# Feed-forward down product: rounds of 2, 2, 2, 2, 3 pairs of feature tiles, operands fetched a round ahead, the residual added by GpSimd

## Chip, cores and metric

One core of one Trainium2 chip runs the whole program. The metric is the device time of one launch in microseconds, lower is better. The trace gives a duration and a releaser for each instruction; TensorE is called PE, VectorE DVE, ScalarE ACT, GpSimd POOL and SyncE SP, as in the trace. SP computes nothing here: it only issues transfers (DMAs), in the order of its program.

## What is computed

The reference is one step of an encoder trunk for 1152 tokens (1024 of a prompt and 8 x 16 of samples) with a model width of 1024. It begins and ends with a half-step feed-forward network:

```
def half_ffn(x, g, w_up, w_down):
    a, b = jnp.split(rmsnorm(x, g) @ w_up, 2, axis=-1)
    return x + 0.5 * ((jax.nn.silu(a) * b) @ w_down)

x <- half_ffn(x, norm_ffn1, ...)
x <- x + token_mix(rmsnorm(x))          # attention and matrix memory, not touched by the change
x <- half_ffn(x, norm_ffn2, ...)
y  = rmsnorm(x)
```

D_FF is 2816, so the hidden layer has 22 tiles of 128 features. The kernel's function `ffn` runs twice; its tensors begin with f1 in the first run and f2 in the second. The change touches both alike.

## The kernel before

**Products.** Every f32 operand is split into a high part and a low remainder, and one product is three matmuls (`product3`, L515 to L519). On top of that a 2 x 2 block product is done with 7 block products instead of 8 (a Strassen scheme). The 1152 tokens form two halves of HT = 576 columns. A tile of weights n therefore has 7 *steps* q = 0 to 6 on PE; each step multiplies one weight block ("slot") by one operand `xd[r, q]` for all 576 columns.

**Up and down.** 22 up tiles come first (n = 0 to 21). They give 11 groups g, each a pair of feature tiles. DVE and ACT pack the 7 operands of each group into `stg` and SP stores them to `h_dram`. Then come 20 down tiles (n = UPS + m, UPS = 22, m = 0 to 19) in five *rounds* of four. All four tiles of a round read the same operands, those of the groups in `ROUNDS[r]`; tile m yields the output rows k = 2(m % 4) and k + 1 of `xT`. Before the change round 0 takes three groups (18 matmuls a step) and the others two (12 matmuls a step). At the end of each step DVE adds the block times 0.5 to `xT` (`accumulate`, L922), which frees the PSUM bank for a later step (`free_bank`): step 4 of tile m = 0, for example, may start when three evictions are done (`dn_ev`).

**Weights.** Per slot ACT writes the high part (`split_hi`, L754) and GpSimd the low part (L872). Four slots are held, so slot x of a tile can be split once PE has done the step four before it. Four of the seven slots need a term that DVE computes (`weight_term`, L893) from the raw weights `raw_d`, of which two tiles are held. `load_raw(n)` on SP therefore waits for the low part of slot 6 of tile n - 2:

```
def load_raw(n):
    sp.wait_ge(lo_ok, slot_no(n - 1, 0))
```

**Order.** Each engine walks the steps in one order written by hand. The tables `RAW_AT`, `LO_AT` (stores), `LOAD_AT` (operands) and `Y_AT` say at which step SP issues what. All is in program order, so an SP wait holds back all later transfers, and a DVE or GpSimd wait all its later work.

**Memory and residual.** The memory of the up operands is 14 pieces of 9216 bytes per partition. An operand of two groups takes one piece, one of three groups one and a half (K3). The input x of the network is saved to `r_dram` at the start, since `xT` serves as scratch during the up stage; `load_y` brings it back in four transfers of 1.18 MB straight into `xT`, and DVE waits for them (`y_in`) before it adds the first block of tiles m = 0 to 3.

Of the kernel before, what the change touches and what calls it, by code (L numbers as in the profile page):

```python
# [20 lines left out]
ALU = mybir.AluOpType  # L21
# [3 lines left out]
P = 128  # L25
# [6 lines left out]
N_TOK = SEQ + DEC_BATCH * DEC_SEQ  # L32
# [4 lines left out]
HT, QT = N_TOK // 2, N_TOK // 4  # L37
# [11 lines left out]
NG = FT // FG  # L49
# [472 lines left out]
def ffn(nc, ctx, M, K, w_up, w_down, gain, xT, xT_at, places, h_dram, r_dram, tag, first, last_io=None):  # L522

    sem = lambda n: ctx.enter_context(nc.semaphore(tag + n))
    UPS, ROUNDS = 2 * NG, ((0, 1, 2), (3, 4), (5, 6), (7, 8), (9, 10))
    DOWNS, RING, STG = 4 * len(ROUNDS), 4, 3
    PACK = (0, 6, 1, 3, 4, 2, 5)
    SOURCE = ((0, 0), (1, 0), 1, 0, 2, (1, 1), 3)
# [3 lines left out]
    def step(n, q):  # L532
        return 8 * n + q if n < 2 else 16 + 7 * (n - 2) + q

    def slot_no(n, x):
        return 4 * n + x if n < 2 else 8 + 7 * (n - 2) + x
# [5 lines left out]
    U_SLOTS, U_STEPS = slot_no(UPS, 0), step(UPS, 0)  # L542
# [14 lines left out]
        COMB_AT[b + (9 if g == 0 else 7)] = (g, 0)  # L557
        COMB_AT[b + (11 if g == 0 else 8)] = (g, 1)
    SUM_HI_AT = {step(0, 7) + e: e for e in range(8)}
    RAW_AT = {step(n, 0) - (6 if n == UPS + 1 else 10 if n > 2 else 12): n for n in range(2, UPS + DOWNS)}  # L560
    assert len(RAW_AT) == UPS + DOWNS - 2
    SQ_STEP = (1, 4, 5, 6)

    main_at, sep_at, raw_at, rhi_at, rlo_at, blk_at = places
    PIECE, K3 = KT // 2 * HT * 4, 3 * HT * 8
    piece = lambda i: main_at + PIECE * i if i < 13 else sep_at
    RING_AT = [K3 * 7 + PIECE * x for x in range(2)] + [sep_at - main_at] + [PIECE * x for x in range(10)]
    OPERAND = {}
    for r, groups in enumerate(ROUNDS):
        for q in range(7):  # L570
            at = K3 * q if r == 0 else RING_AT[(7 * (r - 1) + q) % len(RING_AT)]
            OPERAND[r, q] = main_at + at, len(groups) * HT * 8
    used = [(piece(i), PIECE, step(UPS - 1, i // 2)) for i in range(14)]
    LOAD_AT = {}
    for r in range(len(ROUNDS)):
        for q in range(7):
            at, size = OPERAND[r, q]
            s = max(u[2] for u in used if u[0] < at + size and at < u[0] + u[1])
            LOAD_AT.setdefault(s + 1, []).append((r, q))
            used.append((at, size, step(UPS + 4 * r + 3, q)))  # L580
    Y_AT = {step(UPS, 0) - 3: 0, step(UPS, 0) - 2: 1, step(UPS, 7): 2, step(UPS, 8): 3}
    done_groups = lambda r: sum(len(x) for x in ROUNDS[:r + 1])

    with ExitStack() as mem, M.scope():
# [12 lines left out]
        V = [M.at(f"{tag}v{x}", [P, HT], xT_at + 2 * quarter + x * HT * 4 if x < 2 else blk_at + 2 * HT * 4)  # L597
             for x in range(3)]
        stg = [M.at(f"{tag}stg{x}", [P, 2, HT], xT_at + 2 * quarter + (2 + 2 * x) * HT * 4, F32R) for x in range(STG)]
        sq = [M.at(f"{tag}sq{x}", [P, HT], blk_at + x * HT * 4) for x in range(2)]  # L600
        xs = [(M.at(f"{tag}xs_hi{q}", [P, 4, HT], piece(2 * q), F32R),
               M.at(f"{tag}xs_lo{q}", [P, 4, HT], piece(2 * q + 1), F32R)) for q in range(7)]
# [4 lines left out]
              for r in range(len(ROUNDS)) for q in range(7)}  # L607
        ps = psum(nc, mem, tag + "ps", [P, 8, 512])
        w_in = [sem(f"w_in{x}") for x in range(2)]
        st = [sem(f"st{x}") for x in range(STG)]  # L610
        xd_in = [sem(f"xd_in{q}") for q in range(7)]
        y_in = [sem(f"y_in{x}") for x in range(4)]
        (r_st, t_ok, hi_ok, lo_ok, mm_ok, cp_ok, ad_ok, gl_ok, hm_ok, c_ok, ph_ok, pl_ok, dn_ev, sq_ok, sum_ok) = (
            sem(n) for n in ("r_st", "t_ok", "hi_ok", "lo_ok", "mm_ok", "cp_ok", "ad_ok", "gl_ok", "hm_ok", "c_ok", "ph_ok",
                             "pl_ok", "dn_ev", "sq_ok", "sum_ok"))
        norm = SplitNorm(nc, sem, K, xT, gain, xs, sums, ta, diag, ps, first)
        if last_io is not None:
            z = FinalNorm(nc, sem, K, xT, *last_io, M.at("z_gain", [P, D_MODEL], K["acc_at"]),
# [23 lines left out]
        def source(j):  # L642
            n, x = OWNER[j]
            if n < 2:
                return part(n, x // 2, x % 2)
            return term(n, SOURCE[x]) if isinstance(SOURCE[x], int) else part(n, *SOURCE[x])
# [7 lines left out]
        def w_hi(j):  # L654
            return slot(uw_hi, dw_hi, j)

        def w_lo(j):
            return slot(uw_lo, dw_lo, j)
# [4 lines left out]
        def bank(n, q):  # L663
            if n < 2:
                return ((0, 1, 2, 0), (1, 2, 0, 1))[n][q // 4 * 2 + q % 2]
            return (n - 2 + CHAIN[q]) % 3

        def chain(n, q):
            return ps[:, 2 * bank(n, q):2 * bank(n, q) + 2, 0:QT]

        def pairs(x):
            return x.rearrange("p (i n) -> p i n", i=2)
# [8 lines left out]
        def y_block(m, i):  # L681
            k, t = 2 * (m % 4) + (0, 1, 1, 0)[i], (0, 1, 0, 1)[i]
            return xT[:, k, t * HT:(t + 1) * HT]

        with nc.Block() as block:
            @block.sync
            def _(sp):
                def load_up(n):
                    at = (n // 2) * 2 * P + (D_FF if n % 2 else 0)
                    sp.dma_start(raw_of(n), up_v[:, :, at:at + 2 * P]).then_inc(w_in[n % 2], 16)  # L690

                def load_raw(n):
                    sp.wait_ge(lo_ok, slot_no(n - 1, 0))
                    if n < UPS:
                        load_up(n)
                        return
                    if n == UPS + 1:
                        sp.wait_ge(lo_ok, U_SLOTS)
                    gs, p = round_of(n), (n - UPS) % 4
                    sp.dma_start(raw_of(n), dn_v[:, 2 * gs[0]:2 * gs[-1] + 2, 2 * p * P:2 * (p + 1) * P])\  # L700
                        .then_inc(w_in[n % 2], 16)

                def load_operand(r, q, s):
                    sp.wait_ge(mm_ok, s)
                    if r:
                        sp.wait_ge(xd_in[q], 16 * done_groups(r - 1))
                    for x in range(STG):
                        sp.wait_ge(st[x], 16 * len(range(x, 7 * done_groups(r), STG)))
                    for kk, g in enumerate(ROUNDS[r]):
                        sp.dma_start(xd[r, q][:, kk].bitcast(F32), h_dram.ap()[g, q]).then_inc(xd_in[q], 16)  # L710

                def load_y(x):
                    if x == 0:
                        sp.wait_ge(lo_ok, U_SLOTS)
                    elif x == 1:
                        sp.wait_ge(pl_ok, 7 * (NG - 1))
                    else:
                        sp.wait_ge(pl_ok, 7 * NG)
                        for s in ((0,), (1, 2))[x - 2]:
                            sp.wait_ge(st[s], 16 * len(range(s, 7 * NG, STG)))  # L720
                    sp.wait_ge(r_st, 16)
                    sp.dma_start(xT[:, 2 * x:2 * x + 2], r_dram.ap()[:, 2 * x:2 * x + 2]).then_inc(y_in[x], 16)

                def store(g, i):
                    o = 7 * g + i
                    sp.wait_ge(pl_ok, o + 1)
                    sp.dma_start(h_dram.ap()[g, PACK[i]], stg[o % STG][:].bitcast(F32)).then_inc(st[o % STG], 16)

                load_up(0)
                load_up(1)  # L730
                sp.dma_start(r_dram.ap(), xT[:]).then_inc(r_st, 16)
                for s in range(STEPS):
                    if s in RAW_AT:
                        load_raw(RAW_AT[s])
                    for g, i in LO_AT.get(s, ()):
                        store(g, i)
                    for r, q in LOAD_AT.get(s, ()):
                        load_operand(r, q, s)
                    if s in Y_AT:
                        load_y(Y_AT[s])  # L740
                if last_io is not None:
                    z.load(sp)
                    z.store(sp)
# [123 lines left out]

            @block.gpsimd
            def _(pool):
                for j in range(SLOTS):  # L870
                    pool.wait_ge(hi_ok, j + 1)
                    nc.gpsimd.tensor_tensor(w_lo(j), source(j), w_hi(j).bitcast(F32), ALU.subtract).then_inc(lo_ok, 1)  # L872

            @block.vector
            def _(dve):
                v = nc.vector
# [34 lines left out]
                def accumulate(n, q):  # L911
                    m = n - UPS
                    i = (0, 0, 2, 1, 1, 2, 3)[q]
                    before = 7 * m + {1: 1, 4: 4, 5: 3}[q] if q in (1, 4, 5) else \
                        7 * (m - 4) + {0: 2, 2: 6, 3: 5, 6: 7}[q]
                    dve.wait_ge(mm_ok, step(n, q) + 1)
                    if m < 4 and q == 0:
                        dve.wait_ge(y_in[m], 16)
                    if before > 0:
                        dve.wait_ge(dn_ev, before)  # L920
                    y = pairs(y_block(m, i))
                    v.scalar_tensor_tensor(y, chain(n, q), 0.5, y, ALU.mult, ALU.add).then_inc(dn_ev, 1)  # L922

                def evict(n, q):
# [2246 lines left out]
```

## Time and profile before

| | |
|---|---|
| median of 3 runs | 2591.51 us (2590.43 to 2592.76) |
| profiled execution, its own time | 2589.94 us |
| its span, first to last instruction | 2588.1 us |
| PE busy | 2478.2 us (96%) |
| DVE, ACT, POOL busy | 1629.7, 991.3, 910.0 us (63, 38, 35%) |
| mean granted TensorE clock | 0.974 of 2.4 GHz |
| down stage of f1 | 527.3 to 805.5 us |
| down stage of f2 | 2281.2 to 2560.0 us |

The predictions below are made against the profiled execution's 2589.94 us. Its time is 1.84 us more than its span, and 1.57 us less than the median of the three runs. PE is busy nearly all the time, so time is lost only where PE stands still or runs at its lower clock.

### The profile page before, as it was taken

What the parts mean: (1) busy time and instruction counts of PE and PEld (TensorE: products, weight loads), DVE (VectorE), ACT (ScalarE), POOL (GpSimd) and SP (SyncE); (2) the same over time, 40 slices, a digit from 0 to 9 for tenths busy, and PEclk for the clock granted to TensorE, in tenths of its full rate; (3) what the DMA queues carried; (4) which work ended last, traced back from release to release, by engine and by line L of the source; (5) the groups of instructions that cost most, each with busy time, mean ns of one, the idle gap of its engine ahead of it and who ended that gap; (6) DMA issues with size and microseconds to landing.
All of it is one profiled execution on the core that took longest, in us unless ns stands there. A gap on an engine that the chain in (4) does not pass through costs nothing. (4 is left out here: it accounts for less than half of the span.)

```text
span 2588.1 us, 43001 instructions
## 1 busy us (share of the span) xinstructions
PE 2478.2 (96%) x16970; PEld 2407.1 (93%) x16970; DVE 1629.7 (63%) x2538; ACT 991.3 (38%) x1875; POOL 910.0 (35%) x739
## 2 busy tenths in 40 slices
PE   7999999969998999999998999998999999969997
PEld 7999999969997999999997888998999999969997
DVE  8776767645677237998645643326776766645665
ACT  5443444412234332212557764223444444412223
POOL 1444444424445111112224203411344444424442
PEclk8999999979998999999998999998999999979998
DMA  5243433596544222213334413413333444496552
GB/s 213 107 167 124 147 133 138 182 363 227 200 165 139 54 70 61 68 43 87 103 88 98 63 52 106 152 59 122 115 139 135 142 149 141 148 381 234 188 190 96
DMA packets 226151, 361.46 MB, mean 140 GB/s; under 512 B 39516, under 2 KB 174744, under 8 KB 224544
## 3 DMA queue, kind: packets, MB, share of 16 engines
q1 hardware_dynamic: 225952, 358.72, 40.3%
q8 instruction: 135, 2.21, 0.4%
q14 instruction: 64, 0.52, 0.1%
HBM read 231.21 MB, written 126.26 MB: 138 GB/s over the span
## 5 line engine op out<-in xcount | busy, mean ns | idle before, releaser
L517 PE MATMUL f1ps<-f1xs_lo,f1w_hi 128*128 128x288 f32 x1248 | 369.0, 296 | 3.6 <-DVE f1xs_lo L417 3.6
L517 PE MATMUL f2ps<-f2xs_lo,f2w_hi 128*128 128x288 f32 x1248 | 368.9, 296 | 3.1 <-DVE f2xs_lo L417 3.1
L519 PE MATMUL f1ps<-f1xs_hi,f1w_hi 128*128 128x288 f32 x1248 | 369.2, 296 | 0.0
L519 PE MATMUL f2ps<-f2xs_hi,f2w_hi 128*128 128x288 f32 x1248 | 369.2, 296 | 0.0
L518 PE MATMUL f2ps<-f2xs_hi,f2w_lo 128*128 128x288 f32 x1248 | 368.6, 295 | 0.0
L518 PE MATMUL f1ps<-f1xs_hi,f1w_lo 128*128 128x288 f32 x1248 | 368.6, 295 | 0.0
L517 PE MATMUL d_ps<-xn_lo,d_w_hi 128*128 128x384 f32 x864 | 298.0, 345 | 5.9 <-POOL xn_lo L297 4.3
L518 PE MATMUL d_ps<-xn_hi,d_w_lo 128*128 128x384 f32 x864 | 293.3, 339 | 0.0
L519 PE MATMUL d_ps<-xn_hi,d_w_hi 128*128 128x384 f32 x864 | 293.0, 339 | 0.0
L517 PEld LDWEIGHTS f1ps<-f1xs_lo,f1w_hi 128*128 128x128 f32 x1248 | 235.1, 188 | 5.0 <-POOL f1w_lo L872 4.0
L517 PEld LDWEIGHTS f2ps<-f2xs_lo,f2w_hi 128*128 128x128 f32 x1248 | 235.1, 188 | 4.1 <-issue 3.9
L518 PEld LDWEIGHTS f2ps<-f2xs_hi,f2w_lo 128*128 128x128 f32 x1248 | 235.2, 188 | 0.1
L518 PEld LDWEIGHTS f1ps<-f1xs_hi,f1w_lo 128*128 128x128 f32 x1248 | 235.2, 188 | 0.1
L519 PEld LDWEIGHTS f2ps<-f2xs_hi,f2w_hi 128*128 128x128 f32 x1248 | 235.2, 188 | 0.0
L519 PEld LDWEIGHTS f1ps<-f1xs_hi,f1w_hi 128*128 128x128 f32 x1248 | 235.2, 188 | 0.0
L1552 POOL TENSOR_TENSOR d_w_lo<-d_raw,d_w_hi 128x1024 fp32r<-128x1024 f32 x36 | 87.3, 2424 | 401.6 <-ACT d_w_hi L1417 401.5
L517 PE MATMUL f2ps<-f2xd,f2dw_hi 128*128 128x288 f32 x616 | 184.9, 300 | 25.6 <-issue 22.2
L517 PE MATMUL f1ps<-f1xd,f1dw_hi 128*128 128x288 f32 x616 | 184.5, 299 | 26.0 <-issue 22.0
L1846 DVE TENSOR_SCALAR_CACHE_REDUCE sel_hits<-DM,sel_cand 128x1024 uint8<-128x1024 f32 (+6 forms) x217 | 184.9, 917 | 1.1
L519 PE MATMUL f2ps<-f2xd,f2dw_hi 128*128 128x288 f32 x616 | 184.7, 300 | 0.0
L518 PE MATMUL f2ps<-f2xd,f2dw_lo 128*128 128x288 f32 x616 | 184.4, 299 | 0.0
L519 PE MATMUL f1ps<-f1xd,f1dw_hi 128*128 128x288 f32 x616 | 183.9, 299 | 0.0
(412 smaller groups left out, 6046.4 us busy)
## 6 DMA issues: line engine op xcount, KB each, us to landing
h_dram<-f1stg SPq DMA_DIRECT2D x77, 576.0 KB, 3.3
f1xd<-h_dram SPq DMA_DIRECT2D x77, 576.0 KB, 10.5
h_dram<-f2stg SPq DMA_DIRECT2D x77, 576.0 KB, 3.3
f2xd<-h_dram SPq DMA_DIRECT2D x77, 576.0 KB, 10.9
f1raw<-in_w_ffn_up SPq DMA_DIRECT2D x22, 1024.0 KB, 6.3
f2raw<-in_w_ffn_up SPq DMA_DIRECT2D x22, 1024.0 KB, 6.3
d_raw<-in_w_in SPq DMA_DIRECT2D x35, 512.0 KB, 5.0
p_dram<-stage SPq DMA_DIRECT2D x24, 576.0 KB, 3.4
```

What stands on the lines that cost most here:

```text
L517: nc.tensor.matmul(out, w_hi, x_lo, start=first, stop=False, skip_group_check=onto)
L518: nc.tensor.matmul(out, w_lo, x_hi, start=False, stop=False, skip_group_check=onto)
L519: return nc.tensor.matmul(out, w_hi, x_hi, start=False, stop=final, skip_group_check=onto)
L1552: nc.gpsimd.tensor_tensor(w_lo[:, n0 % 2], raw[:, n0 % 2], w_hi[:, n0 % 2].bitcast(F32), ALU.subtract).then_inc(lo_ok, 1)
L1846: v.tensor_scalar(hits[:, off:off + L], views[j], limit, None, ALU.is_ge, ALU.add, accum_out=cnt[:, j:j + 1]).then_inc(cnt_ok, 1)
```

## The change

Round sizes become 2, 2, 2, 2, 3. Operands of even rounds of two groups use pieces 0 to 6, those of odd rounds pieces 7 to 13, so that a round's operands can be fetched during the round before; from round 1 on they are spread, one for every three steps, and SP waits only for the step that frees the place, not for the step at which the entry stands. `load_raw` of tile UPS + 1 is issued four steps earlier. The first block written to each part of `xT` in round 0 is stored with `tensor_scalar` (times 0.5, nothing added). The residual comes in eight transfers of 0.59 MB (one k each) into two buffers `res`, the e-th issued at step 3 of tile UPS + 5 + e, and GpSimd adds it to `xT[:, k]` after slot 5 of that tile, in program order between the low parts of slots 5 and 6.

```diff
-    UPS, ROUNDS = 2 * NG, ((0, 1, 2), (3, 4), (5, 6), (7, 8), (9, 10))
+    UPS, ROUNDS = 2 * NG, ((0, 1), (2, 3), (4, 5), (6, 7), (8, 9, 10))
...
-    RAW_AT = {step(n, 0) - (6 if n == UPS + 1 else 10 if n > 2 else 12): n for n in range(2, UPS + DOWNS)}
+    RAW_AT = {step(n, 0) - (10 if n > 2 else 12): n for n in range(2, UPS + DOWNS)}
...
-    RING_AT = [K3 * 7 + PIECE * x for x in range(2)] + [sep_at - main_at] + [PIECE * x for x in range(10)]
...
-            at = K3 * q if r == 0 else RING_AT[(7 * (r - 1) + q) % len(RING_AT)]
-            OPERAND[r, q] = main_at + at, len(groups) * HT * 8
+            OPERAND[r, q] = main_at + K3 * q if len(groups) == 3 else piece(7 * (r % 2) + q), len(groups) * HT * 8
...
-            LOAD_AT.setdefault(s + 1, []).append((r, q))
+            LOAD_AT.setdefault(max(s + 1, step(UPS + 4 * r - 4, 3 * q)) if r else s + 1, []).append((r, q, s + 1))
...
-    Y_AT = {step(UPS, 0) - 3: 0, step(UPS, 0) - 2: 1, step(UPS, 7): 2, step(UPS, 8): 3}
+    REST_AT = {step(UPS + 4 + e, 10): e for e in range(8)}
+    ADD_AT = {slot_no(UPS + 5 + e, 5): e for e in range(8)}
...
+        res = [M.at(tag + "res0", [P, N_TOK], K["acc_at"]), M.at(tag + "res1", [P, N_TOK], blk_at)]
...
-                def load_y(x):
-                    if x == 0:
-                        sp.wait_ge(lo_ok, U_SLOTS)
-                    elif x == 1:
-                        sp.wait_ge(pl_ok, 7 * (NG - 1))
+                def load_residual(e):
+                    if e < 2:
+                        sp.wait_ge(r_st, 16)
+                        sp.wait_ge(pl_ok, 7 * NG)
                     else:
-                        sp.wait_ge(pl_ok, 7 * NG)
-                        for s in ((0,), (1, 2))[x - 2]:
-                            sp.wait_ge(st[s], 16 * len(range(s, 7 * NG, STG)))
-                    sp.wait_ge(r_st, 16)
-                    sp.dma_start(xT[:, 2 * x:2 * x + 2], r_dram.ap()[:, 2 * x:2 * x + 2]).then_inc(y_in[x], 16)
+                        sp.wait_ge(ra_ok, e - 1)
+                    k = 2 * (e % 4) + e // 4
+                    sp.dma_start(res[e % 2][:], r_dram.ap()[:, k]).then_inc(y_in[e % 2], 16)
...
+                def add_residual(e):
+                    k = 2 * (e % 4) + e // 4
+                    pool.wait_ge(y_in[e % 2], 16 * (e // 2 + 1))
+                    pool.wait_ge(dn_ev, 7 * (4 + e + 1))
+                    nc.gpsimd.tensor_tensor(xT[:, k], xT[:, k], res[e % 2][:], ALU.add).then_inc(ra_ok, 1)
+
                 for j in range(SLOTS):
                     pool.wait_ge(hi_ok, j + 1)
                     nc.gpsimd.tensor_tensor(w_lo(j), source(j), w_hi(j).bitcast(F32), ALU.subtract).then_inc(lo_ok, 1)
+                    if j in ADD_AT:
+                        add_residual(ADD_AT[j])
...
-                    if m < 4 and q == 0:
-                        dve.wait_ge(y_in[m], 16)
+                    if q == 0 and m == 0:
+                        dve.wait_ge(lo_ok, U_SLOTS)
...
+                    if q == 0 and 8 <= m < 16:
+                        dve.wait_ge(ra_ok, m - 7)
+                    y = pairs(y_block(m, i))
+                    if m < 4 and q in (0, 2, 3, 6):
+                        v.tensor_scalar(y, chain(n, q), 0.5, None, ALU.mult).then_inc(dn_ev, 1)
+                        return
```

SP's program just before the down stage of f1, before the change. `f1draw` is raw_d; `f1xd_312` and the following are the operands of round 0 from q = 4 on; `f1stg` rows are the stores of group 10; the last row loads the raw weights of tile UPS + 1:

```order
L722 DMA xT<-r_dram 128x2304 [waits f1r_st,f1lo_ok]
L710 DMA f1xd_313<-h_dram 128x1152 [waits f1st1,f1st2,f1st0,f1mm_ok]
L710 DMA f1xd_313<-h_dram 128x1152 x2
L722 DMA xT<-r_dram 128x2304 [waits f1r_st,f1pl_ok]
L727 DMA h_dram<-f1stg_285 128x1152 [waits f1pl_ok]
L710 DMA f1xd_314<-h_dram 128x1152 [waits f1st1,f1st2,f1st0,f1mm_ok]
L710 DMA f1xd_314<-h_dram 128x1152 x2
L710 DMA f1xd_315<-h_dram 128x1152 [waits f1st1,f1st0,f1st2,f1xd_in0,f1mm_ok]
L710 DMA f1xd_315<-h_dram 128x1152
L727 DMA h_dram<-f1stg_283 128x1152 [waits f1pl_ok]
```

The same place after the change, from the operand q = 4 of round 0 on (`f1xd_314`):

```order
L710 DMA f1xd_314<-h_dram 128x1152 [waits f1st1,f1st2,f1st0,f1mm_ok]
L710 DMA f1xd_314<-h_dram 128x1152
L710 DMA f1xd_315<-h_dram 128x1152 [waits f1st1,f1st2,f1st0,f1mm_ok]
L710 DMA f1xd_315<-h_dram 128x1152
L700 DMA f1draw<-in_w_ffn_down 128x4x256 [waits f1lo_ok]
L710 DMA f1xd_316<-h_dram 128x1152 [waits f1st1,f1st2,f1st0,f1mm_ok]
L710 DMA f1xd_316<-h_dram 128x1152
L724 DMA h_dram<-f1stg_285 128x1152 [waits f1pl_ok]
L724 DMA h_dram<-f1stg_283 128x1152 [waits f1pl_ok]
L710 DMA f1xd_317<-h_dram 128x1152 [waits f1st1,f1st0,f1st2,f1xd_in0,f1mm_ok]
```

The two transfers into `xT` are gone, and the raw weights of tile UPS + 1 stand ahead of the last operand of round 0, where before they stood after the whole round 0 and the first operands of round 1.

SP's program in the second round after the change; between two loads of raw weights (tiles UPS + 6 and UPS + 7) stand two operands of two transfers each and one residual:

```order
L700 DMA f1draw<-in_w_ffn_down 128x4x256 [waits f1lo_ok]
L710 DMA f1xd_326<-h_dram 128x1152 [waits f1st1,f1st0,f1st2,f1xd_in2,f1mm_ok]
L710 DMA f1xd_326<-h_dram 128x1152
L710 DMA f1xd_327<-h_dram 128x1152 [waits f1st1,f1st0,f1st2,f1xd_in3,f1mm_ok]
L710 DMA f1xd_327<-h_dram 128x1152
L719 DMA f1res_286<-r_dram 128x1152 [waits f1pl_ok,f1r_st]
L700 DMA f1draw<-in_w_ffn_down 128x4x256 [waits f1lo_ok]
```

Here the residual is the last of the transfers that follow a load of raw weights. Among the eight such stretches of a network, five hold four operand transfers, two hold two (e = 2 and 6), and one holds six (e = 7).

GpSimd's program there, tile UPS + 5 after the change (`f1dts_271` is the source of slot 6; the row above the addition is slot 5):

```order
L875 TENSOR_TENSOR f1dw_lo<-f1draw,f1dw_hi 128x256 x2
L875 TENSOR_TENSOR f1dw_lo<-f1dts_269,f1dw_hi 128x256
L875 TENSOR_TENSOR f1dw_lo<-f1dts_268,f1dw_hi 128x256
L875 TENSOR_TENSOR f1dw_lo<-f1dts_270,f1dw_hi 128x256
L875 TENSOR_TENSOR f1dw_lo<-f1draw,f1dw_hi 128x256
L871 TENSOR_TENSOR xT<-xT,f1res_286 128x1152
L875 TENSOR_TENSOR f1dw_lo<-f1dts_271,f1dw_hi 128x256
```

Before the change GpSimd's program has only the `f1dw_lo` rows; the L871 row with its waits is new, and it stands ahead of slot 6.

## Rows read from the trace of the kernel before

**Rows 1.** Waits of PE: engine, line, releaser, us in total, times, longest.

```profile
PE f2ps L517 <- issue: 22.2, 2, 14.6
PE f1ps L517 <- issue: 22.0, 2, 14.4
...
PE f1ps L517 <- DVE xT L922: 4.0, 3, 3.1
```

**Rows 2.** Windows, PE: stretch, length, busy (matmuls), clock, DMA share, GB/s.

```profile
527.30:805.50 278.20, 252.15 (x1851) 0.95 0.56 211
2281.20:2560.00 278.80, 253.19 (x1854) 0.94 0.57 214
```

**Rows 3.** Windows of PE around the first stall of f1.

```profile
533.00:535.00 2.00, 0.00 (x0) 0.94 1.06 431
535.00:537.00 2.00, 0.00 (x0) 0.50 1.00 417
...
545.00:547.00 2.00, 2.00 (x17) 1.00 1.01 415
```

**Rows 4.** Timeline of DVE, f1: start, us, operation [idle before, releaser].

```profile
528.40 1.58 DVE L961 TENSOR_TENSOR f1stg<-f1g,f1stg 128x576 fp32r<-128x576 f32 x1
539.12 0.76 DVE L922 SCALAR_TENSOR_TENSOR xT<-f1ps,xT 128x576 f32<-128x576 f32 x1 [9.13 <-DMA xT<-r_dram]
...
546.38 0.75 DVE L922 SCALAR_TENSOR_TENSOR xT<-f1ps,xT 128x576 f32<-128x576 f32 x1
...
563.86 0.56 DVE L893 TENSOR_TENSOR f1dts<-f1draw 128x384 f32<-128x384 f32 x1 [14.57 <-DMA f1draw<-in_w_ffn_down]
```

**Rows 5.** Timeline of SP, f1, around the first two stalls.

```profile
524.44 0.39 SPq L722 DMA_DIRECT2D xT<-r_dram  x1
...
546.30 1.08 SPq L700 DMA_DIRECT2D f1draw<-in_w_ffn_down  x1
```

**Rows 6.** Timeline of all engines, a steady tile of round 1 of f1.

```profile
675.95 0.38 SPq L700 DMA_DIRECT2D f1draw<-in_w_ffn_down  x1
...
684.73 0.74 POOL L872 TENSOR_TENSOR f1dw_lo<-f1draw,f1dw_hi 128x256 fp32r<-128x256 f32 x1 [0.84 <-ACT f1dw_hi L754]
685.76 0.76 DVE L922 SCALAR_TENSOR_TENSOR xT<-f1ps,xT 128x576 f32<-128x576 f32 x1 [0.84 <-PE f1ps L519]
686.34 0.73 POOL L872 TENSOR_TENSOR f1dw_lo<-f1dts,f1dw_hi 128x256 fp32r<-128x256 f32 x1 [0.88 <-ACT f1dw_hi L754]
687.10 0.38 SPq L700 DMA_DIRECT2D f1draw<-in_w_ffn_down  x1
```

**Rows 7.** Operand transfers 1, 6, 8 of a burst at 607.5: issue, landing.

```profile
L710 SPq DMA_DIRECT2D f1xd<-h_dram x1: 338/338/338, 607.5 to 607.5; - x1
...
L710 SPq DMA_DIRECT2D f1xd<-h_dram x1: 451/451/451, 611.3 to 611.3; - x1
DMA to landing us min/median/max: 7.9/7.9/7.9
...
L710 SPq DMA_DIRECT2D f1xd<-h_dram x1: 446/446/446, 612.7 to 612.7; - x1
DMA to landing us min/median/max: 9.5/9.5/9.5
```

**Rows 8.** The first and the sixth of a burst at 704.9, likewise.

```profile
L710 SPq DMA_DIRECT2D f1xd<-h_dram x1: 339/339/339, 704.9 to 704.9; - x1
...
L710 SPq DMA_DIRECT2D f1xd<-h_dram x1: 433/433/433, 708.5 to 708.5; - x1
DMA to landing us min/median/max: 9.7/9.7/9.7
```

**Rows 9.** GpSimd by shape: count, busy us, mean ns, idle before.

```profile
L1552 POOL TENSOR_TENSOR d_w_lo<-d_raw,d_w_hi 128x1024 fp32r<-128x1024 f32 x36 | 87.3, 2424 | 401.6 <-ACT d_w_hi L1417 401.5
L872 POOL TENSOR_TENSOR f1dw_lo<-f1dts,f1dw_hi 128x256 fp32r<-128x256 f32 x64 | 47.7, 745 | 58.2 <-ACT f1dw_hi L754 58.2
```

More of the change, by code:

```diff
@@ L611, in ffn @@
         xd_in = [sem(f"xd_in{q}") for q in range(7)]
-        y_in = [sem(f"y_in{x}") for x in range(4)]
-        (r_st, t_ok, hi_ok, lo_ok, mm_ok, cp_ok, ad_ok, gl_ok, hm_ok, c_ok, ph_ok, pl_ok, dn_ev, sq_ok, sum_ok) = (
+        y_in = [sem(f"y_in{x}") for x in range(2)]
+        (r_st, t_ok, hi_ok, lo_ok, mm_ok, cp_ok, ad_ok, gl_ok, hm_ok, c_ok, ph_ok, pl_ok, dn_ev, sq_ok, sum_ok, ra_ok) = (
             sem(n) for n in ("r_st", "t_ok", "hi_ok", "lo_ok", "mm_ok", "cp_ok", "ad_ok", "gl_ok", "hm_ok", "c_ok", "ph_ok",
-                             "pl_ok", "dn_ev", "sq_ok", "sum_ok"))
+                             "pl_ok", "dn_ev", "sq_ok", "sum_ok", "ra_ok"))
         norm = SplitNorm(nc, sem, K, xT, gain, xs, sums, ta, diag, ps, first)
@@ L736, in _ @@
                         store(g, i)
[L737 to L740, printed above, removed]
+                    for r, q, free in LOAD_AT.get(s, ()):
+                        load_operand(r, q, free)
+                    if s in REST_AT:
+                        load_residual(REST_AT[s])
                 if last_io is not None:
@@ L916, in accumulate @@
                     dve.wait_ge(mm_ok, step(n, q) + 1)
-                    if m < 4 and q == 0:
-                        dve.wait_ge(y_in[m], 16)
+                    if q == 0 and m == 0:
+                        dve.wait_ge(lo_ok, U_SLOTS)
+                    if q == 0 and m in (2, 3):
+                        for x in ((0,), (1, 2))[m - 2]:
+                            dve.wait_ge(st[x], 16 * len(range(x, 7 * NG, STG)))
+                    if q == 0 and 8 <= m < 16:
[4 more added lines that the diff above has]
+                        return
                     if before > 0:
                         dve.wait_ge(dn_ev, before)
-                    y = pairs(y_block(m, i))
                     v.scalar_tensor_tensor(y, chain(n, q), 0.5, y, ALU.mult, ALU.add).then_inc(dn_ev, 1)
```

## The prediction

> **What bounds the kernel now.** I read first who PE waits for, then windows of the down stages, then the timelines of DVE, SP and GpSimd there. PE is the bound: in a steady tile of two groups the raw weights are loaded every 11.15 us (675.95 to 687.10, [rows 6]), which is PE's pace of 84 matmuls; a step of 12 takes 1.59 us. At that pace the down stage of a network, 16 tiles of two groups and 4 of three, takes 16 x 11.15 + 4 x 1.5 x 11.15 = 245.3 us. It takes 278.2 and 278.8 us by the windows [rows 2], whose edges hold up to a microsecond of other work. So each network loses about 32 us, which is all that a better order of the down stage can give.
>
> Where they go: the two "issue" waits are 22.0 us in f1 and 22.2 in f2, and f1 loses another 4.0 behind evictions [rows 1] (f2's comes to about the same). The first one, 7.6 us: DVE has finished a packing at 529.98, then stands 9.13 us for the residual, issued at 524.44 and landed at 539.0 behind the operands of round 0 [rows 4, 5]. The second, 14.4 us: DVE stands 14.57 us for raw weights issued at 546.30 and landed at 563.8, because they were queued behind everything else [rows 4, 5]. During the first stall the granted clock falls from 1.00 (2.4 GHz) to 0.50 (1.2 GHz) and is back only in the stretch that starts at 545 [rows 3]; PE resumed at 540, so 5 us ran at half speed and 2.5 us are lost. The second costs about as much. 22 + 4 + 5 is 31, the rest is small gaps. Take **32 us a network**.
>
> **What the change removes.** The 4.72 MB of residual leave the crowded stretch, round 0 needs 14 operand transfers instead of 21, and the raw weights of tile UPS + 1 stand ahead of its last operand. Both DMA waits of DVE go. The third stall, 3.1 us at the start of round 1, also came from raw weights behind a burst of operands; with two operands between two loads of raw weights it goes too. Three groups in the last round give the squares there 2.4 us a step and remove the last 0.9 us in f1. I count the whole 32 us as removed, then add what comes instead.
>
> **What it adds in round 0.** The number of evictions stays 140 a network, and a first block stored with a multiplication alone costs what the eviction in its place cost, 0.76 us from PSUM [rows 4]; at most some tenths less, so zero. But PE now needs 1.59 us a step and not 2.39, while DVE still packs group 10 in tile m = 0. Step 4 needs three evictions. Before, from the start of the first eviction (539.12) to that of the third (546.38) DVE worked through 7.26 us without a pause [rows 4]; with terms of 256 columns it is about 0.6 less. It can begin at 529.8, so the third eviction ends at 529.8 + 6.7 + 0.75 = 537.2. PE, begun at 527.3, would be at step 4 at 533.7: a stall of 3.5 us. Two terms and one packing ahead of the fifth eviction cost about 1.1 us more at step 6. A stall of 3.5 us is between the 3.1 us one, after which no clock was lost, and the 7.6 us one that cost 2.5; I add 1.0. **5.6 us**, from 3 (packings overlap better) to 9 (both stalls with the clock).
>
> **What it adds in rounds 1 and 2.** This decides. GpSimd's addition stands between slots 5 and 6 of a tile. In the steady tile [rows 6] slot 5's low part ends at 685.47, and PE, whose step 2 ended at 685.76, starts step 6 three steps later, at 690.5. In these 5.1 us must fit: the wait for the residual, the addition, and slot 6's low part, 0.75 [rows 9]. The addition is 128x1152: 128x1024 takes 2.42 and 128x256 0.745, thus 2.19 ns a column, 2.42 + 0.28 = 2.70 us [rows 9]. DVE's evictions from PSUM do not stretch GpSimd's work, and when the addition runs late DVE is idle, so I take 2.70. The residual may land at most 1.6 us after slot 5, at 687.1, which is 11.1 us after the raw load at 675.95.
>
> The residual is the last of a burst: raw weights, four operand transfers, residual. A burst of like transfers whose waits were all satisfied landed its sixth at 611.3 + 7.9, that is 11.7 us after its first issue, and its eighth at 14.7 [rows 7]; a second burst landed the sixth after 13.3 us [rows 8]. The raw weights are 0.52 and not 0.59 MB, 0.2 us less; the range is 11.5 to 13.1, and I take 11.7, nearer to the first, since SP's waits are satisfied here too. So the first residual is 0.6 us too late: hardly a loss. But `load_raw` waits for slot 6 of the tile before, and that slot now ends behind the addition. Every burst then starts when the previous addition and slot 6 are done, and holds the residual for which the next addition waits. That is a closed loop: landing of the residual, 0.1 us, addition 2.70, low part 0.75, next raw load; 3.6 us besides the landing. With four operand transfers it takes 11.7 + 3.6 = 15.3 us a tile, where PE needs 11.15.
>
> For the eight residuals, with 3.0 us less where there are two operand transfers and 3.0 more where there are six (the spacing of 1.5 us from the sixth to the eighth, [rows 7]): landings 5 x 11.7 + 2 x 8.7 + 14.7 = 90.6, plus 8 x 3.6 = 28.8, plus 0.1 to PE: 119.5 us from the raw load to PE's step 6 of tile UPS + 12. Unchanged it would be 8 x 11.15 + 3.4 = 92.6. **Loss 26.9 us a network.** The clock's falls within the loop cost nothing, as PE waits anyway; after the last and longest wait, 7 us, it costs 2.5. Bounds: at 431 GB/s, the highest rate in [rows 3], 3.47 MB take 8.1 us, and with two thirds of the 3.5 us that the first burst took beyond that rate the landing is 10.4, a loss of 17.5; at 13.3 it is 39.7.
>
> The Trainium skill, "DMA: Bandwidth & Descriptors", section "Where 436 GB/s comes from", says that transfers between HBM and SBUF are bound by about 358 GB/s a core. The trace does not agree: 407 to 431 GB/s stood for many microseconds. By that rule a transfer would take 1.65 us instead of 1.5, and the sum would be about 12 us higher for both networks.
>
> **Sum.** A network: -32 + 5.6 + 26.9 + 2.5 = +3.0; both: +6 us on the profiled execution's own 2589.94: **2596 us**. Its time is 1.6 us below the median of the runs, which is within the spread.
>
> **Rivals.**
> 1. *The residual is in time* (0.10). The loop exists only if a landing plus 3.6 us exceeds 11.15, so below 7.6 us. For it speaks that a single operand transfer lands in about 4 us, if the residual were served beside the others; against it that landings in a burst come in the order of issue, 1.5 us apart. Then -32 + 5.6 = -26.4 a network, 2537 us: clearly faster.
> 2. *Bursts land like the second one* (0.10), because transfers of different kinds, or the restart after each idle stretch, slow them. At 13.3 us and more a network loses 39.7 + 2.5 + 5.6 - 32 = +15.8: 2621 us. This is also the direction of the rule on HBM.
> 3. *The forecast* (0.80): 2572 to 2617 us for landings of 10.4 to 13 and 3 to 9 us in round 0. It holds both signs; its centre is 0.24% above the kernel before.
> The new operand order itself hurting (a piece freed too late) I give nothing of its own: in round 4 the operand of q = 4 is issued after step 1 of the tile before and needed ten steps later, over 15 us.
>
> **How the numbers follow.** What a measurement can tell from no change is about 0.2%, 5.2 us. Of the forecast's 0.80 I put 0.20 below that, 0.22 within, 0.38 above. Faster: 0.20 + 0.10 = 0.30; same 0.22; slower 0.38 + 0.10 = 0.48. The range is 2572 to 2617, which leaves out rival 1 and part of rival 2.
>
> **What the profile of the changed kernel would show.** PE without waits for "issue" of 7 and 14 us at the start of the down stage, but with one of 3 to 4 us about 6 us after it. From tile UPS + 6 on PE waits of about 4 us before step 6, released by GpSimd's slot 6, and GpSimd's additions waiting for the residual's DMA by several microseconds; SP's raw loads 15 us apart and not 11.15; the last wait about 7 us. DMA to landing of the residual 8 to 10 us. If the additions wait less than 1.6 us and PE does not stand at step 6, rival 1 holds, and the step that failed is the landing or the loop. If the waits are there but 5 to 6 us long, rival 2. If DVE is seen behind in round 0 by more than 5 us, the term of 5.6 is too small.

## Result: 0.18% slower, and 58 us found behind one queue order

The changed kernel takes 2594.9 us in the median of 16 runs, the kernel before 2590.64; the ratio is 1.0018 (95% interval 1.0011 to 1.0026). The profiled execution took 2596.77 us (span 2595.0) against 2589.94, so +6.8 us where the prediction's sum said +6. In the trace PE's last matmul of the down stage starts 3.7 us later than before in f1 (808.93 against 805.19) and the final norm's first transpose 7.7 us later (2568.78 against 2561.05), so 4.0 us are added behind f1.

The waits of PE (engine, line, releaser, us in total, times, longest), in the changed kernel:

```profile
PE f1ps L517 <- POOL f1dw_lo L875: 16.4, 5, 6.7
PE f2ps L517 <- POOL f2dw_lo L875: 15.8, 4, 6.6
...
PE f2ps L517 <- DVE xT L935: 5.6, 5, 2.1
PE f1ps L517 <- issue: 4.8, 2, 2.8
PE f1ps L517 <- DVE xT L935: 4.6, 4, 2.1
...
PE f2ps L517 <- issue: 2.8, 1, 2.8
```

Of the 22 us a network for "issue" in [rows 1], 2.8 us at step 4 of the first down tile are left, and in f1 another 2.1 at its step 6. In their place PE waits 16 us a network for GpSimd's low part (L875, that was L872) and 5 us for evictions. The busiest new row of the chain that ended last is a DMA: `f2res<-r_dram`, 3% of the span.

SP's timeline in the second round of f1:

```profile
585.18 0.38 SPq L700 DMA_DIRECT2D f1draw<-in_w_ffn_down  x1
585.73 1.83 SPq L710 DMA_DIRECT2D f1xd<-h_dram  x4
587.67 0.37 SPq L719 DMA_DIRECT2D f1res<-r_dram  x1
600.74 0.38 SPq L700 DMA_DIRECT2D f1draw<-in_w_ffn_down  x1
...
616.27 0.38 SPq L700 DMA_DIRECT2D f1draw<-in_w_ffn_down  x1
616.83 0.85 SPq L710 DMA_DIRECT2D f1xd<-h_dram  x2
617.72 0.43 SPq L719 DMA_DIRECT2D f1res<-r_dram  x1
628.69 0.38 SPq L700 DMA_DIRECT2D f1draw<-in_w_ffn_down  x1
...
704.65 0.38 SPq L700 DMA_DIRECT2D f1draw<-in_w_ffn_down  x1
```

The raw loads, 11.15 us apart in [rows 6], are 14.3 to 15.7 us apart in f1 where four operand transfers lie between them, 12.4 and 13.5 where there are two, and 18.1 where there are six. From the first row to the last, eight residuals, are 119.47 us; the prediction had 119.4. In f2 they are 122.6 us (2341.37 to 2463.99), where one cycle alone was 16.86 us long. GpSimd's timeline shows what each cycle waits for:

```profile
607.41 0.73 POOL L875 TENSOR_TENSOR f1dw_lo<-f1draw,f1dw_hi 128x256 fp32r<-128x256 f32 x1 [0.83 <-ACT f1dw_hi L751]
612.95 2.61 POOL L871 TENSOR_TENSOR xT<-xT,f1res 128x1152 f32<-128x1152 f32 x1 [4.81 <-DMA f1res<-r_dram]
615.52 0.72 POOL L875 TENSOR_TENSOR f1dw_lo<-f1dts,f1dw_hi 128x256 fp32r<-128x256 f32 x1
```

Slot 5's low part is ready at 608.14; then GpSimd stands 4.81 us for the residual, adds for 2.61 us, and slot 6 ends at 616.24. SP's next raw load is at 616.27. All eight additions of f1 waited for their residual, 30.4 us together.

```profile
L871 POOL TENSOR_TENSOR xT<-xT,f1res x8: 2607/2680/2881, 597.2 to 701.3; 128x1152 f32<-128x1152 f32 x8
  DMA f1res<-r_dram: 30.4, 8
DMA to landing us min/median/max: 7.3/8.8/10.6
```

(These are the rows on the tile `f1res`: its instructions in ns, what GpSimd waited for, and the landings from the residual's own issue.) The last residual's landing is 690.70 + 10.6, 14.75 us after its raw load at 686.55.

PE's own waits are smaller than what the loop costs. Between 590 and 720 us of f1 PE stands 20.8 us (16.4 behind GpSimd, 4.4 behind evictions), while the eight cycles take 26.9 us more than at PE's pace. By the granted clock of windows of 2 us, about 4.7 us of the difference are lost to work at 1.2 GHz after these waits (0.56 and 0.58 of 2.4 GHz from 617 to 621, 0.50 from 645 to 647 and from 659 to 661, and parts of three more windows).

### The profile page after: what moved, and what is told of

Read it like the earlier page. It is cut to its first block and busy times, and to the rows that moved or that the text cites. A ratio compares the mean times of both kernels' runs of the same rounds, so it can differ in the third digit from the quotient of the medians.

```text
span 2595.0 us, 43033 instructions
## 1 busy us (share of the span) xinstructions
PE 2482.4 (96%) x16970; PEld 2411.0 (93%) x16970; DVE 1638.4 (63%) x2538; ACT 991.7 (38%) x1875; POOL 956.5 (37%) x755
## 5 line engine op out<-in xcount | busy, mean ns | idle before, releaser
L517 PE MATMUL f1ps<-f1xd,f1dw_hi 128*128 128x288 f32 x616 | 186.2, 302 | 25.8 <-POOL f1dw_lo L875 16.4
```

The source lines that it names most:

```text
L517: nc.tensor.matmul(out, w_hi, x_lo, start=first, stop=False, skip_group_check=onto)
```

## Experiments

All times are medians. Each kernel ran beside the kernel before on the same chip; ratios are against it. The kernels ran in three groups, in which the kernel before took 2590.8, 2589.6 and 2589.4 us.

### Residual ahead of the operands: res_first

```diff
-    REST_AT = {step(UPS + 4 + e, 10): e for e in range(8)}
+    REST_AT = {step(UPS + 4 + e, 4): e for e in range(8)}
...
+                    if s in REST_AT:
+                        load_residual(REST_AT[s])
                     for r, q, free in LOAD_AT.get(s, ()):
                         load_operand(r, q, free)
-                    if s in REST_AT:
-                        load_residual(REST_AT[s])
```

> The changed kernel with each residual transfer issued right behind the raw weights, ahead of the operand transfers, and not after them. The loop theory (the addition waits for a residual that is last in a burst, and the next burst waits for the addition) expects the residual to land about 5 us after the raw load instead of 11.7, in time for GpSimd, no wait of PE before step 6, and raw loads 11.2 us apart: 2595 minus twice (26.9 + 2.5), about 2536 us. The rival that the addition itself costs the time (2.7 us of GpSimd, and DVE blocked meanwhile) expects no change, about 2595 us.

Measured 2536.36 us, ratio 0.9788 (0.9773 to 0.9803). Rows on `f1res` of this kernel:

```profile
L871 POOL TENSOR_TENSOR xT<-xT,f1res x8: 2672/2682/2695, 593.8 to 671.8; 128x1152 f32<-128x1152 f32 x8
DMA to landing us min/median/max: 4.5/4.5/4.9
```

No row for a wait stands between them any more; the additions start 11.1 us apart (78.0 us for seven), PE's pace. The order of two issues on SP is worth 58.5 us (the prediction's loop with its clock term is twice 29.4, 58.8), and the rival that the addition itself costs the time falls.

### The addition two slots later: add_later, and with the earlier residual: first_later

```diff
-    ADD_AT = {slot_no(UPS + 5 + e, 5): e for e in range(8)}
+    ADD_AT = {slot_no(UPS + 6 + e, 0): e for e in range(8)}
```

> The changed kernel with the addition placed two slots later, after slot 0 of the next tile; the transfers stay in their order. The loop theory expects the same gain as from the earlier transfer, about 2536 us, although the residual still lands 11 to 12 us after the raw load: the raw load no longer stands behind the addition, and GpSimd comes to it 3.2 us later. Only the residual behind six operand transfers may cost some tenths. A theory in which a late landing alone costs the time expects half of the loss to stay, about 2565 us; the rival of the addition's own cost expects 2595 us.

Measured 2575.64 us, ratio 0.9939 (0.9924 to 0.9954), 40 us more than expected. I had not foreseen why. Here no addition waited for a DMA and the raw loads did not stand behind it. But VectorE did something new, by its timeline in this kernel:

```profile
596.21 0.90 DVE L898 TENSOR_TENSOR f1dts<-f1draw 128x256 f32<-128x256 f32 x1
597.24 2.66 DVE L898 TENSOR_TENSOR f1dts<-f1draw,f1dts 128x256 f32<-128x256 f32 x1
599.82 0.74 DVE L935 SCALAR_TENSOR_TENSOR xT<-f1ps,xT 128x576 f32<-128x576 f32 x1
...
603.97 0.76 DVE L935 SCALAR_TENSOR_TENSOR xT<-f1ps,xT 128x576 f32<-128x576 f32 x1 [2.40 <-PE f1ps L519]
```

GpSimd's addition runs there from 596.78 to 599.61. The second weight term, 0.42 us when alone, ends with it and takes 2.66; the eviction behind it is late, and PE stands 2.0 us: 12.4 us in seven waits behind L935 and 4.0 in two behind GpSimd, a network. The Trainium skill, "SBUF — State Buffer", section "SBUF: two separate sides", says that of a GpSimd operation that reads SBUF and a VectorE operation with two SBUF inputs the one that starts second is blocked until the first is done. The trace agrees: the term ends 0.29 us after the addition. The evictions, whose one input is in PSUM, keep their 0.74 to 0.76 us.

> Both moves together: the residual's transfer ahead of the operands and the addition behind slot 0 of the next tile. In the trace with the later addition alone no addition waited for a DMA, but DVE's second weight term (step 3 of the tile) took 2.66 us beside the 2.83 us addition and PE stood 2.0 us for the eviction behind it. If that collision is the whole cost, the residual's place in the queue does not matter here and the time stays at 2575 us. If the late landing had a part in it, the time falls to 2536 us.

Measured 2579.38 us, ratio 0.9958 (0.9943 to 0.9972), 3.7 us above add_later, which I did not trace. With the residual landed 4.7 us after its issue PE's waits are the same 12.4 and 4.0 us, so a late landing had no part in them. In f1 of add_later the clock falls twice behind these waits (0.50 from 601 to 603 and from 683 to 685), some 3 us lost. Together that is about the 20 us a network by which add_later lies above res_first.

### Only the addition moved, to a place where VectorE has no such work: add_next4

```diff
-    ADD_AT = {slot_no(UPS + 5 + e, 5): e for e in range(8)}
+    ADD_AT = {slot_no(UPS + 6 + e, 4): e for e in range(8)}
```

> The changed kernel with all its transfers in their order, and only the addition moved: behind slot 4 of the next tile. There it starts about 3 us after that tile's first step and should end before VectorE's two weight terms at the end of step 3. The loop theory with the collision on the port as the second cause expects both costs gone: the residual still lands 11 to 12 us after the raw load, GpSimd does not wait, VectorE's terms take no 2.7 us, and the time is 2536 to 2540 us. If a late transfer or GpSimd's 2.7 us themselves cost anything, it stays at 2560 us or above.

Measured 2535.27 us, ratio 0.9793 (0.9777 to 0.981). Rows on `f1res`:

```profile
L871 POOL TENSOR_TENSOR xT<-xT,f1res x8: 2672/2676/2688, 602.2 to 680.7; 128x1152 f32<-128x1152 f32 x8
DMA to landing us min/median/max: 6.7/9.5/11.4
```

The residuals land as late as in the changed kernel, or later, and GpSimd adds just as long. Nothing of the 60 us between this kernel and the changed one is left. This separates the loop from its parts: neither the late landing nor the 2.7 us cost anything by themselves.

### A place between: res_mid

```diff
-    REST_AT = {step(UPS + 4 + e, 10): e for e in range(8)}
+    REST_AT = {min(s for s in LOAD_AT if s >= step(UPS + 4 + e, 4)): e for e in range(8)}
+    assert len(REST_AT) == 8
```

> The changed kernel with each residual transfer behind the first operand of its burst (fourth transfer after the raw weights' load begins; fifth where an operand has three groups), a place between the two tried. The loop theory gives a cycle of 8.7 + 3.6 = 12.3 us a residual (13.8 for the last) against 11.15 that PE needs: over eight residuals 99.9 + 0.1 - 92.6, so 7 us a network, with little lost to the clock: about 2536 + 14 = 2550 us, raw loads 12.3 us apart, residual landing about 7 us after its issue. A theory without the closed loop, in which each residual is late for itself alone, has 8.7 us inside the 11.1 that are free and expects 2536 us.

Measured 2555.76 us, ratio 0.9864 (0.9849 to 0.988); the four runs spread from 2549.83, the profiled one, to 2559.27. The first and the last raw load of the eight cycles:

```profile
584.19 0.38 SPq L701 DMA_DIRECT2D f1draw<-in_w_ffn_down  x1
...
683.80 0.38 SPq L701 DMA_DIRECT2D f1draw<-in_w_ffn_down  x1
```

99.6 us against 99.9 expected, and the same in f2; the median landing in f1 is 7.0 us. So the length of the closed loop is confirmed, and a theory without it (2536) is out. The median time is 6 us above the expectation; additions that run beside weight terms delay evictions here too (PE waits 3.1 us in f1 and 5.0 in f2 behind L936), which may be part of it, but I did not separate that.

### The residual in another engine's queue: act_queue

```diff
-    REST_AT = {step(UPS + 4 + e, 10): e for e in range(8)}
+    REST_AT = {step(UPS + 4 + e, 4): e for e in range(8)}
...
-                    sp.dma_start(res[e % 2][:], r_dram.ap()[:, k]).then_inc(y_in[e % 2], 16)
...
+                    act.dma_start(res[e % 2][:], r_dram.ap()[:, k]).then_inc(y_in[e % 2], 16)
...
+                    if s in REST_AT:
+                        load_residual(REST_AT[s])
```

> The changed kernel with the residual transfers issued by ScalarE (after step 4 of the tile before, about 2 us later than SP's raw load) and not by SP. If what makes the residual late is its place behind the operands in SP's queue, the other queue lets it land about 4 to 7 us after its issue, inside the 9 us that are free, and the time is 2536 to 2545 us. If the two queues share nothing but bandwidth and the residual still lands after all bytes issued before it, it comes 9 us after its issue, the loop stays in part, and the time is 2565 to 2590 us.

Measured 2538.28 us, ratio 0.9804 (0.9787 to 0.982). The time is the one expected for the case in which the place in the queue decides, but seven of the eight residuals do not test that. ScalarE issues only the first of a network behind SP's transfers and all others ahead of SP's next raw load:

```profile
583.80 0.38 SPq L700 DMA_DIRECT2D f1draw<-in_w_ffn_down  x1
584.35 1.82 SPq L710 DMA_DIRECT2D f1xd<-h_dram  x4
585.78 0.35 ACTq L817 DMA_DIRECT2D f1res<-r_dram  x1
596.93 0.33 ACTq L817 DMA_DIRECT2D f1res<-r_dram  x1
597.37 0.38 SPq L700 DMA_DIRECT2D f1draw<-in_w_ffn_down  x1
```

The seven that go first land 4.2 to 4.7 us after their issue in f1; in res_first it is 4.5 to 4.9. The first, behind the burst, takes 7.9 us, and in the changed kernel it took 9.4. So the other queue cuts the loop here mainly by issuing earlier; what it does for a transfer issued behind a burst is seen once a network, and is smaller.

### Neither transfer nor addition: no_res

```diff
-                    if s in REST_AT:
-                        load_residual(REST_AT[s])
...
-                    if j in ADD_AT:
-                        add_residual(ADD_AT[j])
```

> The changed kernel without the residual: neither its transfers nor GpSimd's additions (the output lacks the residual of both networks). It measures what the rounds and the fetching ahead give by themselves. The loop theory expects about 2536 us, no less than the two kernels in which the residual is in time; the rival of the addition's own cost expects it to be the only one that fast, with the other two near 2595.

Measured 2538.68 us, ratio 0.9797 (0.9781 to 0.9813), no faster than the kernels that do add the residual in time. (The wait of VectorE for the addition is left out with it.) The change without its residual gives 52 us; the residual costs nothing when it is well placed.

### The rounds: old_rounds and first_old

```diff
-    UPS, ROUNDS = 2 * NG, ((0, 1), (2, 3), (4, 5), (6, 7), (8, 9, 10))
+    UPS, ROUNDS = 2 * NG, ((0, 1, 2), (3, 4), (5, 6), (7, 8), (9, 10))
```

> The changed kernel with the old round sizes 3, 2, 2, 2, 2. The stall of 5 us at step 4 and 6 of the first tile goes, as PE takes 2.4 us a step there. But operands 0 to 3 of round 1 lie where the last operands of round 0 are read until its last two steps, so eight transfers come late: by spacings of 1.5 us the fourth operand lands 7.6 us after PE wants it, and the clock costs up to 2.5 more. Expected 2595 minus 2 x 5 plus 2 x 10, about 2605 us. If the order of rounds does not matter, it is within 3 us of 2595.

Measured 2609.86 us, ratio 1.0071 (1.0056 to 1.0086), where about 2605 was expected; PE waits 6.9 us in f1 and 7.1 in f2 for the operands' transfers.

> The kernel with the residual ahead of the operands and the old round sizes 3, 2, 2, 2, 2. It separates the rounds from the residual: without the closed loop the round sizes should cost what the operands' late landing costs, 6.9 to 7.1 us of PE waiting for their DMA in the trace of the old rounds, and 2.5 for the clock, less the 2.8 and 2.5 at the start: about 4 us a network, 2544 us in all. If the old rounds cost more because of the loop, as 2610 against 2595 would suggest, 2551 us.

The same edit on res_first: 2557.1 us, ratio 0.9874 (0.9859 to 0.9889), 13 us above the expectation. PE's waits in f1 of first_old:

```profile
PE f1ps L517 <- DMA f1xd<-h_dram: 8.1, 5, 3.1
PE f1ps L517 <- DVE xT L935: 3.9, 3, 3.0
```

The operands' late landing is there as expected; I had left out the 3.0 us behind an eviction at the turn of the round (3.4 in f2), which is half of the miss, and did not trace the rest. The old sizes cost 20.7 us over res_first (2536.4) and 15.0 over the changed kernel. So the loop does not make the old sizes dearer; beside it they cost rather less, which no run explains.

### The early load of raw weights: raw_back

```diff
-    RAW_AT = {step(n, 0) - (10 if n > 2 else 12): n for n in range(2, UPS + DOWNS)}
+    RAW_AT = {step(n, 0) - (6 if n == UPS + 1 else 10 if n > 2 else 12): n for n in range(2, UPS + DOWNS)}
```

(The edit is made to res_first.)

> The kernel with the residual ahead of the operands, and the raw weights of the second down tile back at their old place in the order, four steps later. Only the move of this load is undone. The trace of before had its stall of 14 us there, but with far more in the queue; now about 9 transfers of 1.5 us lie ahead at 531, so it should land near 541, 2 us after VectorE wants it: 2536 plus 2 x 2 to 3, about 2541 us. If the smaller first round alone had removed the stall, no change from 2536.

Measured 2540.96 us, ratio 0.9811 (0.9797 to 0.9826), on res_first's 2536.4. The load is issued at 533.54 and lands 9.1 us later, at 542.6:

```profile
542.66 0.43 DVE L898 TENSOR_TENSOR f1dts<-f1draw 128x256 f32<-128x256 f32 x1 [3.52 <-DMA f1draw<-in_w_ffn_down]
```

VectorE stands 3.52 us and PE 2.7 more than in res_first (1.2 in f2). So this one line is worth 2.3 us a network, and most of the former 14 us stall went with the rest of the change (the smaller first round, the residual that left it, the operands of round 1 that are fetched later), whose parts no run separates.

### Less for VectorE before step 4: comb_late

```diff
-        COMB_AT[b + (11 if g == 0 else 8)] = (g, 1)
+        COMB_AT[b + (11 if g == 0 else 9 if g == NG - 1 else 8)] = (g, 1)
...
-        for i, e in enumerate((-4, -4, 0 if late else -3, 1 if late else -1)):
+        for i, e in enumerate((-4, -4, 0 if late else -3, 2 if late else -1)):
```

(The edit is made to res_first.)

> The kernel with the residual ahead of the operands, and besides the second combination of group 10 and the last weight term of the first down tile one step later on VectorE, behind the third eviction. The stall of 2.8 us at step 4 (and the 2.5 us of half clock that follow it) should shrink to under 1 us, but the work returns before steps 5 and 6, where up to 2 us may be lost: from 2536 to about 2532 us, or no change if the later steps take it all back.

Measured 2538.79 us, ratio 0.9799 (0.9784 to 0.9814), not to be told from res_first. PE's one wait of 2.8 us for "issue" has become two, 4.1 us together, 2.1 the longest: the work returned at once. That VectorE's amount of work bounds the first tile, and not its order, is likely from this, but one reordering does not show it.

## Why the prediction was right

**The kernel before could give 32 us a network.** Held. Without the residual (no_res) and with the addition at another place (add_next4) 52 and 54 us are gained, 26 and 27 a network; the first rival, which took what the first tile keeps off the 32, gave 26.4 (2537 us). With some 5 us of round 0 put back, that is 31 to 32.

**The two waits for a DMA go.** Held: no wait for `xT<-r_dram` is left, and none for raw weights.

**The evictions that now multiply only.** 0.74 us in the trace, against 0.76 [rows 4]; nothing, as taken.

**Round 0, 5.6 us a network.** Place and mechanism held. The timeline of VectorE in the changed kernel:

```profile
529.37 0.74 DVE L931 TENSOR_SCALAR xT<-f1ps 128x576 f32<-128x576 f32 x1
...
535.77 0.74 DVE L931 TENSOR_SCALAR xT<-f1ps 128x576 f32<-128x576 f32 x1
```

The first eviction starts at 529.37 (foreseen 529.8) and the third at 535.77 and not 536.5; PE waits 2.77 us and not 3.5. The second wait in f1 came where it was foreseen, before step 6: PE resumes at 542.10, when the fifth eviction (541.26, 0.74 us) is done. It was 2.07 us and not 1.1. The clock, given 1.0, fell once in f1:

```profile
541.00:543.00 2.00, 0.90 (x4) 0.79 1.02 353
543.00:545.00 2.00, 2.00 (x10) 0.50 1.08 348
545.00:547.00 2.00, 2.00 (x15) 0.86 0.89 269
```

(Windows of PE: stretch, length, busy (matmuls), granted clock, DMA share, GB/s.) About 3.5 us at 1.2 GHz are some 1.8 us lost. f1 comes to 2.8 + 2.1 + 1.8 = 6.7 us. f2 has the first wait alone, 2.8 us, but there the clock fell at once:

```profile
2292.00:2294.00 2.00, 0.13 (x1) 0.16 (x1) 2.00 (x4) 0.43 (x2) 1.14 (x2) 0.80 1.03 424
2294.00:2296.00 2.00, 2.00 (x9) 2.00 (x10) 2.00 (x4) 1.66 (x3) 1.98 (x2) 0.50 1.02 422
...
2298.00:2300.00 2.00, 2.00 (x10) 2.00 (x9) 1.37 (x2) 0.33 (x1) 0.42 (x1) 0.50 1.02 406
2300.00:2302.00 2.00, 2.00 (x16) 2.00 (x16) 1.74 (x3) 0.91 (x3) 1.26 (x1) 1.00 1.05 411
```

(The same columns, with those of PEld, DVE, ACT and POOL behind PE's.) Six us at 0.50 are 3 us lost, so f2 comes to 5.8. Both are near the 5.6, by another division of it.

**The closed loop, 26.9 us a network.** This term decided. Its length held to 0.1 us in f1 (119.47 against 119.4) and was 3.2 us short in f2 (122.6). So close a hit in f1 is in part luck: single cycles are up to 1.2 us longer (13.50 for 12.3) and 1.0 shorter (14.29 for 15.3) than foreseen, and these cancel. Over both networks the residuals behind four operands landed 10.6 to 13.5 us after their raw load, in the mean the 11.7 that was taken. The last landing in f1 was 14.75 us after its raw load for 14.7 (15.7 in f2); addition 2.68 in the median for 2.70. The loop's cause is shown by kernels that cut it at different places, the order of issue (res_first) and GpSimd's order (add_next4), and by one that shortens it (res_mid).

**PE's waits in the loop.** Foreseen were about 4 us before step 6 in each tile and 7 at the end. Measured in f1 are 1.9 to 3.1 us in four tiles behind GpSimd and 0.5 to 2.1 in three behind evictions, then 6.7. The period held, but PE spends part of it on work at 1.2 GHz instead of standing, as said with the result.

**"When the addition runs late DVE is idle."** Wrong, without a price in this kernel. Five of f1's eight additions met a weight term, which then took 1.3 to 2.9 us; the first:

```profile
597.25 2.88 DVE L898 TENSOR_TENSOR f1dts<-f1draw 128x256 f32<-128x256 f32 x1
```

It is 0.89 us in the tiles before the loop. PE's 2.09 us wait behind L935, which ends at 601.81, comes from it. But every addition waited for its transfer, none for VectorE, so the loop's length did not depend on these meetings. Taken alone they are dear: 40 us in add_later.

**The clock after the last wait, 2.5 us.** The clock falls at about 703 and is back by 709.2, so 4.5 us of work at 1.2 GHz, 2.3 us lost. **Rival 2** (bursts that land in 13.3 us) was the exception: one of the ten bursts with four operands took so long, in f2 (13.5 us, the cycle of 16.86), the other nine at most 12.2. The rate of 358 GB/s did not bind: windows here again show 419 to 424 GB/s.

**The range and the chances.** One bound was mis-added: at a landing of 10.4 us the loss is 26.9 - 8 x 1.3 = 16.5 us and not 17.5, so the lower end would be 2570. The upper end, 2617, is a landing of 13 us with 5.6 us in round 0; with the 9 us named it would be 2624. Neither changes how 2595 lies in it. In the sum a network gains 32 us and pays 35, so the sign of so small a remainder was not safe, and the prediction said so. By its own measure of 0.2% the 4.3 us are "the same", to which it gave 0.22, and not the slower kernel, to which it gave 0.48, though the interval of the ratio excludes 1.

## What to carry to other kernels

When a transfer is consumed by an engine whose next product also releases the next burst, the transfer's place in that burst sets a period: add up landing, consumer and release, and compare the sum with the pace of the bound engine. Cut the loop where it is cheapest, by issuing first what is needed first, or by letting the consumer run behind the instruction that releases the burst. And give a long GpSimd operation a stretch in which VectorE has no operation with two SBUF inputs: the same 2.7 us cost nothing at one slot and 2.5 us each at another.

## What the runs showed of the hardware

In act_queue the first residual of f1 was issued by ScalarE at 585.78, behind 2.9 MB that SP had issued since 583.80. It landed after 7.9 us, at 593.7. The last of SP's four operand transfers, issued just before it, landed after 10.1 us, at 595.8, where the transfer at the same place took 8.6 us in the changed kernel. So two queues are served side by side, each at the other's cost, and a transfer in the other queue does not have to wait for all bytes issued before it. It is the only case in f1; in f2 the residual took 8.6 us and that operand 10.2.

In the changed kernel the granted clock stayed at 1.00 (2.4 GHz) in the windows from 533 to 539, around the 2.8 us wait of f1's first tile, and was 0.50 (1.2 GHz) from 2294 to 2300, after the same wait in f2; in res_first it was 0.50 from 537 to 541, in f1. The same idle time at the same place does not always have the same price, and no run here shows what decides it.
